# Delta rule's front: sums of squares in column strips, gate rows as transposes, gate projection in four fp32 strips

## What is computed

```python
proj = h @ w_in                      # (512, 1024) @ (1024, 4112): q, k, v, z, b_raw, a_raw
qkv = silu(causal_dwconv(qkv, conv_w))
q = l2_normalize(q) * (128 ** -0.5)  # x * rsqrt(sum(x * x) + 1e-6), for each of 8 heads of 128
k = l2_normalize(k)
beta = sigmoid(b_raw)
g = -exp(a_log) * softplus(a_raw + dt_bias)
# chunks: here of 128 tokens, of each of 8 heads
G = cumsum(g)
decay = exp(G[:, None] - G[None, :])         # lower triangle
L = strict_lower((beta * k) @ k.T * decay)
u, w = solve(I + L, beta * v), solve(I + L, beta * k * exp(G))
# then a scan over the chunks with the state of each head
```

## Time and profile before

| | |
|---|---|
| median of three runs | 1375.21 us |
| span of the profiled execution | 1374.7 us |
| TensorE matmul busy | 1316.5 us (96%) |
| VectorE busy | 823.7 us (60%) |
| ScalarE busy | 569.7 us (41%) |
| GpSimd busy | 126.3 us (9%) |
| TensorE clock, mean of the span | 0.987 of full |

### The profile page before, as it was taken

The page is one execution under the profiler, slowest core; times in us unless marked ns, Lnnn a source line. Parts: engine busy times, 40 slices in busy tenths (PEclk is TensorE's granted clock), DMA queues, the critical chain, the costliest instruction groups (busy, mean ns, idle before and its releaser), DMA issues. The chain is left out here.

```text
span 1374.7 us, 18203 instructions
## 1 busy us (share of the span) xinstructions
PE 1316.5 (96%) x7011; PEld 1080.8 (79%) x7011; DVE 823.7 (60%) x1436; ACT 569.7 (41%) x1085; POOL 126.3 (9%) x142
## 2 busy tenths in 40 slices
PE   3799999999999999999999999999999999999998
PEld 3668788889798888888888866656888888888886
DVE  4879787557577655665656769776463323333335
ACT  3356674555453212221224665675353213222231
POOL 1002020005300000000000011130000000000000
PEclk9899999999999999999999999999999999999999
DMA  9644522110516555564532211010122223322321
GB/s 323 203 159 149 184 66 89 63 62 4 182 62 231 200 180 184 184 214 154 184 125 90 84 33 33 30 62 1 62 92 92 92 92 118 97 92 70 115 92 62
DMA packets 102856, 158.39 MB, mean 115 GB/s; under 512 B 9325, under 2 KB 74106, under 8 KB 102778
## 3 DMA queue, kind: packets, MB, share of 16 engines
q1 hardware_dynamic: 91898, 115.40, 25.6%
q0 software_dynamic: 10880, 41.95, 8.9%
HBM read 155.24 MB, written 2.10 MB: 114 GB/s over the span
## 5 line engine op out<-in xcount | busy, mean ns | idle before, releaser
L401 PE MATMUL ps<-h_hi,w_hi 128*128 128x512 f32 x872 | 344.6, 395 | 0.4 <-ACT tmp L1054 0.4
L403 PE MATMUL ps<-h_hi,w_lo 128*128 128x512 f32 x872 | 341.4, 391 | 0.0
L402 PE MATMUL ps<-h_lo,w_hi 128*128 128x512 f32 x872 | 341.1, 391 | 0.0
L385 DVE TENSOR_TENSOR w_lo<-raw,w_hi 128x1024 fp32r<-128x1024 f32 x172 | 209.4, 1223 | 210.6 <-ACT w_hi L379 208.9
L379 ACT ACTIVATE w_hi<-raw 128x1024 fp32r<-128x1024 f32 x174 | 182.4, 1051 | 142.6 <-PE ps L2083 137.3
L403 PEld LDWEIGHTS ps<-h_hi,w_lo 128*128 128x128 f32 x872 | 164.7, 189 | 35.0
L401 PEld LDWEIGHTS ps<-h_hi,w_hi 128*128 128x128 f32 x872 | 164.9, 189 | 33.7 <-issue 0.5
L402 PEld LDWEIGHTS ps<-h_lo,w_hi 128*128 128x128 f32 x872 | 165.0, 189 | 33.5
L504 DVE SCALAR_TENSOR_TENSOR ada_acc<-ada_in,c_act,ada_acc 128x512 f32<-128x512 f32 x154 | 115.5, 750 | 4.2
L1944 ACT ACTIVATE g_hi<-tmp 128x512 fp32r<-128x512 f32 x44 | 27.8, 632 | 201.0 <-DVE tmp L1979 201.0
L2081 PE MATMUL ps<-w_hi,g_hi 128*128 128x512 f32 x256 | 100.1, 391 | 0.0
(11 more groups left out here) (387 smaller groups left out, 2145.4 us busy)
## 6 DMA issues: line engine op xcount, KB each, us to landing
raw<-in_ffn_w_in_dram SPq DMA_DIRECT2D x44, 1024.0 KB, 5.2
ada_in<-in_ada_w_dram POOLq DMA_DIRECT2D x40, 1024.0 KB, 5.6
raw<-in_ffn_w_out_dram SPq DMA_DIRECT2D x20, 1024.0 KB, 5.0
raw<-in_gdn_w_in_dram SPq DMA_DIRECT2D x16, 1024.0 KB, 5.8
ada_in<-in_ada_w_dram SPq DMA_DIRECT2D x4, 1024.0 KB, 9.5
x_t<-in_x_dram SPq DMA_DIRECT2D x2, 2048.0 KB, 10.0
early_slab<-in_ada_w_dram SPq DMA_DIRECT2D x4, 1024.0 KB, 14.3
raw<-in_gdn_w_out_dram SPq DMA_DIRECT2D x4, 1024.0 KB, 4.9
```

The lines of the kernel that those rows point to most:

```text
L385: ops.tensor_tensor(lo, raw_tile(s, kc) if src is None else src, f32(hi), ALU.subtract).then_inc(lo_done, 1)
L401: nc.tensor.matmul(out_, hi[:, k, :], r_hi[:, k, :], start=k == 0, stop=False)
L402: nc.tensor.matmul(out_, hi[:, k, :], r_lo[:, k, :], start=False, stop=False)
L403: last = nc.tensor.matmul(out_, lo[:, k, :], r_hi[:, k, :], start=False, stop=k == kc - 1)
```

## The change

- Sums of squares: the squares of eight key heads get eight places in `eu`, those of the queries three. Four (three, two) heads are summed at once: for each head one fp32 matmul with 32 stationary columns (`picker`: ones in column g, zeros elsewhere) and 512 moving columns, into its own quarter of PSUM's partitions, so that it uses its own strip of 32 columns of the array. Keys: groups in slots 5 and 9; queries: slots 28, 31 and behind the loop. The sums then lie along the free dimension; ScalarE copies them out, four transposes turn them (slot 10; queries: in the state loop behind unit 0), and VectorE reads them.
- VectorE's reading of the key sums moves from the head of its slot 10 to the end of it, the factors likewise in slot 11. The reading of the query sums moves from ahead of the state loop into its second turn.
- Query squares are made one slot later, the last one at the start of ScalarE's state loop, behind `act_cb`.
- Gate rows: instead of a matmul a transpose of the repeated column of G itself, which needs the sums that VectorE takes over in slot 7. TensorE's wait for g becomes a wait for those.
- Gates: 16 fp32 matmuls in four strips, weights unsplit and padded from 16 to 32 columns, the high and the low half of h as fp32; VectorE adds the four parts (three additions more). The rounding and subtraction of the weights go.
- GpSimd clears `ba_raw` and makes `picker`; SP waits for the first constants ahead of the small loads.

The diff, cut to its core:

```diff
-        sq_ring = [diag[:, :, :].rearrange("p a b -> p (a b)"), tmp[:, 2, :]]
+        k_squares = [flat(eu[:, 4 * j:4 * j + 4, :]) for j in range(H)]
+        q_squares = [diag[:, :, :].rearrange("p a b -> p (a b)"), tmp[:, 2, :], ada_acc[:, :]]
+        K_GROUPS, Q_GROUPS = [(0, 1, 2, 3), (4, 5, 6, 7)], [(0, 1, 2), (3, 4, 5), (6, 7)]
...
+        def act_q_square(act, j):
+            n = TO_QUERIES + j
             act.wait_ge(sem("qkv_made"), convolved(n))
+            if j == 0:
+                act.wait_ge(sem("k_turned"), 1)
+            if j >= 3:
+                act.wait_ge(sem("qk_sum"), 2 + j // 3)
+            nc.scalar.activation(q_squares[j % 3], qkv[:, channel(n), :], ACT.Square).then_inc(sem("qk_sq"), 1)
+        def pe_sums(pe, squares, groups, g, first):
+            pe.wait_ge(sem("qk_sq"), first + groups[g][-1] + 1)
...
+            for j, h in enumerate(groups[g]):
+                last = nc.tensor.matmul(ps[32 * j:32 * j + 32, 4, :], picker[:, g, :], squares[h % len(squares)],
+                                        start=g == 0, stop=g == len(groups) - 1, skip_group_check=True)
+            last.then_inc(sem("qk_sum"), 1)
+        def act_sums_out(act, dst, signal, sums):
+            act.wait_ge(sem("qk_sum"), sums)
+            nc.scalar.activation(dst, ps[:, 4, :], ACT.Copy).then_inc(sem(signal), 1)
+        def pe_sums_turn(pe, src, ready, signal):
+            pe.wait_ge(sem(ready), 1)
             for b in range(NB):
-                last = nc.tensor.matmul(ps[:, 4, j * NB + b:j * NB + b + 1], sq_ring[j % 2][:, b * P:(b + 1) * P],
-                                        ones[:, 0:1], start=True, stop=True)
-            last.then_inc(sem("qk_sum"), 1)
+                last = nc.tensor.transpose(ps[:, 4, b * P:(b + 1) * P], src[:, b * P:(b + 1) * P], ident[:, :])
+            last.then_inc(sem(signal), 1)
...
         def pe_gates(pe):
-            pe.wait_ge(sem("ba_split"), 1)
-            for k in range(DC):
-                nc.tensor.matmul(ps[0:2 * H, 6, :], ba_hi[:, k, :], h_hi[:, k, :], start=k == 0, stop=False)
...
+            for i, h in enumerate((h_hi, h_lo)):
+                for half_ in range(2):
+                    for j in range(4):
+                        k = 2 * j + half_
+                        last = nc.tensor.matmul(ps[32 * j:32 * j + 32, 6, :], ba_raw[:, k, :], f32(h[:, k, :]),
+                                                start=i == 0 and half_ == 0, stop=i == 1 and half_ == 1,
+                                                skip_group_check=True)
...
         def pe_grow(pe, m):
             if m == 0:
-                pe.wait_ge(sem("small_made"), 1)
+                pe.wait_ge(sem("g_sums_made"), 1)
...
-                last = nc.tensor.matmul(heads_of(2 + m % 2)[:, h, :], column(gate, m, h).to_broadcast([P, P]),
-                                        upto[:, :], start=True, stop=True)
+                last = nc.tensor.transpose(heads_of(2 + m % 2)[:, h, :],
+                                           column(gsum[:, 0, :, :], m, h).to_broadcast([P, P]), ident[:, :])
...
         def gdn_slot_act(act, n):
-            if n < TO_VALUES or n >= TO_QUERIES:
-                act_square_of(act, n)
+            if n < TO_VALUES:
+                act_k_square(act, n)
+            if n > TO_QUERIES:
+                act_q_square(act, n - 1 - TO_QUERIES)
+            if n == 9:
+                act_sums_out(act, k_sums_at, "k_sums_out", 2)
...
         def gdn_slot_dve(dve, ch, n):
-            if n == 10:
-                dve_k_sums(dve)
-            if n == 11:
-                dve_factors(dve, ch)
             if n == 13:
                 dve_negc(dve)
             dve_ada_slot(dve, ch, n)
...
                 out_split(dve, nc.vector, 0, Q_GDN_OUT, n % 4)
+            if n == 10:
+                dve_k_sums(dve)
+            if n == 11:
+                dve_factors(dve, ch)
...
         def gdn_slot_pe(pe, n):
-            if 2 <= n < 10:
-                pe_sum_of(pe, n - 2)
+            if n in (5, 9):
+                pe_sums(pe, k_squares, K_GROUPS, n // 4 - 1, 0)
+            if n == 10:
+                pe_sums_turn(pe, k_sums_at, "k_sums_out", "k_turned")
...
-            if n >= 26:
-                pe_sum_of(pe, n - 18)
+            if n in (28, 31):
+                pe_sums(pe, q_squares, Q_GROUPS, (n - 28) // 3, H)
...
         def states_act(act):
+            act_q_square(act, H - 1)
             kg_out(act, 0)
...
                 u_out(act, m)
+                if m == 0:
+                    act_sums_out(act, q_sums_at, "q_sums_out", len(K_GROUPS) + len(Q_GROUPS))
```

More of the change, by code:

```diff
@@ L1093, in pe_gates, with act_k_square @@
-        def pe_gates(pe):
-            pe.wait_ge(sem("ba_split"), 1)
-            for k in range(DC):
-                nc.tensor.matmul(ps[0:2 * H, 6, :], ba_hi[:, k, :], h_hi[:, k, :], start=k == 0, stop=False)
-                nc.tensor.matmul(ps[0:2 * H, 6, :], ba_hi[:, k, :], h_lo[:, k, :], start=False, stop=False)
-                last = nc.tensor.matmul(ps[0:2 * H, 6, :], ba_lo[:, k, :], h_hi[:, k, :],
-                                        start=False, stop=k == DC - 1)
+        def act_k_square(act, j):
+            act.wait_ge(sem("qkv_made"), convolved(j))
+            if j == H - 1:
+                act.wait_ge(sem("small_turned"), 1)
+            nc.scalar.activation(k_squares[j], qkv[:, channel(j), :], ACT.Square).then_inc(sem("qk_sq"), 1)
@@ new lines, in head_sums @@
+        def head_sums(groups, g):
+            return ps[:, 4, :].rearrange("p (b j r) -> p b j r", b=NB, r=32)[:, :, 0:len(groups[g]), g]
+        def pe_gates(pe):
+            pe.wait_ge(sem("misc_in"), 16 * N_MISC)
+            for i, h in enumerate((h_hi, h_lo)):
[5 more added lines that the diff above has]
+                                                skip_group_check=True)
@@ L1121, in dve_gates_in @@
             dve.wait_ge(sem("small_turned"), 1)
-            ch(nc.vector.tensor_copy(ba[:, :, :], ps[:, 5, 0:NB * 2 * H].rearrange("p (a b) -> p a b", a=NB)))
+            parts = ps[:, 5, :].rearrange("p (b j n) -> p b j n", b=NB, j=4)
+            ch(nc.vector.tensor_copy(ba[:, :, :], parts[:, :, 0, 0:2 * H]))
+            for j in range(1, 4):
+                ch(tt(ba[:, :, :], ba[:, :, :], parts[:, :, j, 0:2 * H], ALU.add))
             ch(tt(a_in, a_in, dt_b[:, 0, :].unsqueeze(1).to_broadcast([P, NB, H]), ALU.add))
@@ L1197, in dve_k_sums @@
         def dve_k_sums(dve):
-            dve.wait_ge(sem("qk_sum"), H)
-            nc.vector.tensor_scalar(k_r[:, :, :], ps[:, 4, 0:NB * H].rearrange("p (h b) -> p b h", b=NB),
-                                    EPS, None, ALU.add).then_inc(sem("small_sum"), 1)
+            dve.wait_ge(sem("k_turned"), 1)
+            for g in range(2):
+                nc.vector.tensor_scalar(k_r[:, :, 4 * g:4 * g + 4], head_sums(K_GROUPS, g), EPS, None, ALU.add)\
+                    .then_inc(sem("k_sums"), 1)
         def pool_k_root(pool):
-            pool.wait_ge(sem("small_sum"), 1)
+            pool.wait_ge(sem("k_sums"), 2)
             nc.gpsimd.tensor_tensor(k_r[:, :, :], k_r[:, :, :], half[:, 0:NB * H].rearrange("p (a b) -> p a b", a=NB),
@@ L1221, in dve_q_sums @@
         def dve_q_sums(dve):
[L1223 to L1225 removed]
+            dve.wait_ge(sem("q_turned"), 1)
+            for g, heads in enumerate(Q_GROUPS):
+                nc.vector.tensor_scalar(q_eps[:, :, heads[0]:heads[-1] + 1], head_sums(Q_GROUPS, g), EPS, P * EPS,
+                                        ALU.add, ALU.mult).then_inc(sem("q_sums"), 1)
         def act_eb(act, m):
@@ L1730, in states_dve @@
                     r_of(dve, m)
+                if m == 1:
+                    dve_q_sums(dve)
+                    dve.wait_ge(sem("q_sums"), len(Q_GROUPS))
                 if m:
@@ L2669, in _ @@
             pool_first_root(pool)
+            ch(nc.gpsimd.memset(picker[:, :, :], 0.0))
+            for g in range(3):
+                ch(nc.gpsimd.memset(picker[:, g, g:g + 1], 1.0))
             fill(upto[:, :], 1.0, (ALU.is_ge, 0.0, 0, [[1, P]], -1))
```

51 lines of the change are left out of this document (20 added, 31 removed).

## The result

The changed kernel takes 1382.44 us (median of four runs, 1381.46 to 1384.17) beside 1375.61 for the kernel before in the same session: a ratio of 1.0049 with a 95% interval of 1.0037 to 1.0062. It is slower by 6.8 us, on the forecast's side and inside its range, with a size of 6.8 where 4.3 was said.

The account below looks back on a forecast made before the run. Bounds: TensorE's queue, a chain from key sums over GpSimd, a slab transfer and VectorE to tile 15, and early VectorE's slots. 5.6 - 3.9 + 1.6 + 0.4 + 0.6 = +4.3, plus 0.5 on 1374.7: 1379.5 us, range 1375 to 1384.

Parts of the forecast that it names:

- The bounds: TensorE's queue; the chain from key sums over GpSimd, a transfer and VectorE to tile 15; before tile 6, VectorE's slots.
- part 3: Key sums read 5.6 us later, at 137.0; roots, slab, product of L and tile 15 follow: +5.6 up to tile 26.
- part 2: Gate rows wait for gate sums: TensorE stands 4 us, rows 0.9 shorter, tile 10 about 0.5 us earlier.
- The two stands: TensorE waits at tile 14 and at the product of L, some 7 us; sign: 3 to 5 us behind tile 14.
- Part 1: Up to the gates' turn: VectorE moves 2.4 us earlier, TensorE stands about 5, clock costs 0.5, gain kept 1.9.
- The clock term: Half clock: +1.7 for the second stand in part 3, against a stretch behind tile 26 perhaps going; net +0.6, bounds -1.7 to +3.4.
- Part 4: Query sums: seven sums before the state loop become two groups, -3.9; last group worse placed +1.6; query sums' turn +0.4.
- The stretch of rows 10: Half clock behind tile 26 after small tiles and a sum; it may go, -1.7, two thirds taken.
- The tail: End of the query sums: last square and group come later, scaled keys at 295.7, +1.6, TensorE's state loop waits.
- Rival (a): fp32 strips run only two abreast, a group costs 2.0 us: +4.5, 1384; chance 0.15.
- Rival (b): Later reading costs nothing because GpSimd's root and the slab are covered: -3.8, 1371.4; chance 0.16.
- Rival (c): TensorE's queue is all that counts: -12.6, 1362.6; chance 0.04.

Follow-up runs that it names:

- e3: Kernel before with only VectorE's reading of the key sums moved to the end of slot 10 and the factors to the end of slot 11: 1382.07 us.
- e1: Changed kernel with GpSimd issuing adaLN slab 8 ahead of the roots of the key sums instead of behind them: 1370.91 us.
- e11: Kernel before with only the change's gate projection (four fp32 strips, read-out and transposes, three added sums, no weight split): 1375.98 us.
- e8: Changed kernel with seven fp32 matmuls that nobody reads, put where TensorE stands 6.5 us for the first product of L: 1379.65 us.
- e6: Changed kernel with ScalarE's last query square ahead of the two small copies in the last slot, as in the kernel before: 1383.51 us.
- e7: Changed kernel with slab 8 issued ahead of the roots, first two units of gate rows as old matmuls, last query square ahead of the copies: 1366.68 us.
- e9: e2 with one fp32 matmul of 512 columns that nobody reads, ahead of the half inverses, where TensorE stood 1.1 us: 1375.05 us.
- e2: Kernel before with GpSimd issuing adaLN slab 8 ahead of the roots of the key sums: 1378.41 us.

## Why the prediction was right, and where it was short

**The bounds and part 3** were right, and are shown: e3 makes the loss by the move alone, and e1 takes it away by the order of GpSimd's queue alone. The size holds too: in e3 the slab and the product of L come 5.5 later, counted from the gates' turn, for the 5.6 of the forecast. In the changed kernel the key sums were read at 138.24, not 137.0, which is part 2's doing. The two stands, put at 7 us together, were 2.51 and 6.52, the second above the 3 to 5 that were named as a sign. That e3 and the whole change lose the same is partly luck: e3 has none of the 3.9 us that the change takes off the query sums, and in the changed kernel these went to the clock.

**Part 1** held in its sum (-1.75 for -1.9) and the stand (5.04 for 5), and its reason held as well. It let VectorE move by the 2.4 us of its wait and no further. With the gates' product alone (e11) VectorE still waits 0.54 and the stand stays at 2.00; in the changed kernel, where the sums ahead are gone too, VectorE doesn't wait there any more and the stand grows to 5.04. It was e11's own expectation that had this wrong. The close fit of the 1.75 is partly luck: over all profiles of the two fronts the gates' turn is 2.6 earlier on average.

**Part 2**: a wait of 3.2, released by the gate sums, for 4. Its pieces do not add up to its result. Rows that start at 117.3 instead of 117.19 and are 0.9 shorter, and a slot 9 that is 0.6 shorter, make tile 10 start 1.4 earlier, where it says 0.5; the 0.9 between them is named nowhere, and the clock, bounded there at 0 to 1.7, is the only item without a value. Measured, the gate sums were written at 117.80 instead of 117.3, and half clock took all of 1.7: the first rows took 1.37 us from start to start where later ones took 0.8, and tile 9 took 6.74 for 5.57. So tile 10 starts 0.75 later than before, and the key sums come 1.2 later than forecast.

**The clock term** is the one that was mis-sized. Without it the forecast's parts come to +3.3 at the scaled keys; measured are +8.4, and the 5.1 between them lie in three places. VectorE's work on the slab is 0.9 later than forecast (the 1.2 above, less 0.4 by which the roots took less). From there to tile 26 another 1.25 is lost, mostly since the stretch from 166 to 176 us takes in the product's matmuls (3.40 us from start to start, 2.31 before, 1.78 in e8). And from tile 26 to the scaled keys 2.95 are lost (part 4). The forecast had 0.6 for all of it, from what 3 us at half clock lost. Stretches came where it said, and one where it had put a gain, but they were 7 and 10 us long. The medians, which are 1.1 nearer to each other than the profiled executions, leave some 3 for this term (6.8 less the 3.7 of the others). How much of it hangs on which stand is shown only for the one at the product, 1.7 in e8's profile.

**Part 4**: the saving is real but was not paid out in the changed kernel. From tile 26 to tile 31 it takes 44.1 us for 44.8 before; e1 takes 41.0 and e8 41.0. The stretch of rows 10 did go, as the forecast had thought likely (-1.1), and won 1.5, but a longer one came at 261: the half inverses took 5.84 us for 3.94, the tile behind them 6.84 for 5.66, and a stand of 1.2 lay ahead. So some 3 of the 3.9 us were lost. e1 and e8 show that this stretch need not come. The tail was +1.4 against tile 31's read-out for +1.6. But e6 moved it and won nothing, so as a term of the median it is not confirmed.

**Rival (a)**, strips two abreast, is refuted by the starts 10 ns apart at 276.46 and by the group's 1.00 us. The Trainium skill's 2.38x for three column tiles (TensorE: Matmul & The Clock Gate, Part 3) would have given an estimated 1.08 plus the seams; the trace has 0.99 with the seams in it. The measurement decides. **Rival (b)**, the slab covered, did not happen, but e1 made it happen: 1370.9, beside the 1371.4 worked out for it, with tile 15 2.4 earlier than before for the 1.9 there. **Rival (c)** is refuted by the result itself; e7, without the late slab, still stays 4 us above its 1362.6.

## What to carry to other kernels

When a read is moved later, follow not only who needs its value but what else is queued behind the instruction that needs it: here a transfer that has nothing to do with the key sums stood behind their roots, and swapping the two made the same change a gain. Price a stand of TensorE by its length and by the work that may follow it at half clock. Where TensorE sets the pace, a matmul that nobody reads can be worth more than it costs (3.4 us in e9); behind the gates' turn the medians show no gain. And before a difference between two profiles is explained, look how far apart they are already ahead of the change.

## What the runs showed of the hardware

- In e2 a stand of 1.11 us, behind 24 matmuls of 512 columns and ahead of 64 of 64x64, was followed by 10.2 us at half clock with TensorE busy throughout; with 0.24 us in its place there was none (e9). A stand of 1.1 to 1.3 us at the same place was followed by half clock in four profiles and by full clock in six.
- Three fp32 matmuls of 32 stationary and 512 moving columns in their own column strips start 10 ns apart and run side by side; four strips need 1.00 us, three 0.99, entry and exit included.
- GpSimd's power on 32 columns took between 5.46 and 6.03 us, with the same shape: 5.90 before, 5.46 in the changed kernel, and 6.03 and 5.47 in e2 and e9, which are alike up to there. What the difference hangs on is open.
